# Where the large on-chip tensors begin: a two-layer decoder trunk with its SBUF tensors moved by 128 or 192 bytes

## What is computed

```python
for i in range(DEPTH):                       # DEPTH = 2, layer i
    shift1, scale1, gate1, shift2, scale2, gate2 = split(silu(c) @ w_mod[i] + b_mod[i], 6)
    h = rms_norm(x, g0) * (1 + scale1) + shift1
    y = pool_mixer(h) if i == 0 else diff_attention(h)
    x = x + gate1 * rms_norm(y, g1)
    h = rms_norm(x, g2) * (1 + scale2) + shift2
    if i == 0: y = (silu(h @ w_g) * (h @ w_u)) @ w_down              # width 2816
    else:      y = sum over 8 experts e of gate[e] * swiglu_e(h)      # width 3584 each
    x = x + gate2 * rms_norm(y, g3)
```

## Time and profile before

| | us |
|---|---|
| three runs | 1496.49, 1496.77, 1496.89 (median 1496.77) |
| the profiled execution, device time | 1496.16 |
| its span, first to last instruction | 1493.9 |
| PE busy | 1374.5 (92% of the span) |
| DVE busy | 1204.4 (81%) |
| ACT busy | 891.3 (60%) |
| DMA | 465.12 MB, 311 GB/s over the span |

### The profile page before, as it was taken

How to read it: one execution, slowest core, us unless ns; L and a number is a source line. 1 busy time by engine, 2 the same in 40 slices (tenths; PEclk the granted TensorE clock), 3 DMA queues, 4 the chain that set the end, 5 groups by cost and what they waited for, 6 DMA issues and landing times.

```text
span 1493.9 us, 19719 instructions
## 1 busy us (share of the span) xinstructions
PE 1374.5 (92%) x6868; PEld 1133.7 (76%) x6868; DVE 1204.4 (81%) x951; ACT 891.3 (60%) x726; POOL 46.9 (3%) x56
## 2 busy tenths in 40 slices
PE   0559999989778999999999999999999999999995
PEld 0349999779557888788788878878887887887883
DVE  7777677788767888888888888888888888888883
ACT  1144433444745776676677767667776766766771
POOL 2230000000200000000000000000000000000000
PEclk9969999999988999999999999999999999999998
DMA  9978788859137999999999999999999999999970
GB/s 375 372 235 296 253 308 289 288 191 393 35 115 245 375 368 337 337 365 364 333 337 370 331 335 367 353 335 354 367 333 337 364 335 335 364 368 334 336 294 30
DMA packets 206228, 465.12 MB, mean 311 GB/s; under 512 B 14472, under 2 KB 37072, under 8 KB 206176
## 3 DMA queue, kind: packets, MB, share of 16 engines
q1 hardware_dynamic: 203744, 456.19, 85.1%
q0 software_dynamic: 2432, 8.26, 1.6%
HBM read 463.33 MB, written 1.06 MB: 311 GB/s over the span
## 4 chain that ended last, share of the span: by engine, by line
PE 85%; DVE 8%; issue 2%; DMA 2%; ACT 1%; POOL 1%; POOLq 0%; DVEq 0%; SPq 0%; ACTq 0%
PE ps L1263 26%; PE ps L1265 26%; PE ps L1264 26%; DVE rows L860 2%; PE ps L1503 2%; PE ps L1512 2%; DVE rows L862 2%; PE ps L1529 2%; DMA raw<-w_mod 1%; DVE wlo L848 1%; PE ps L1247 1%; PE ps L1258 1%; ACT whi L584 1%; DVE ysb L922 0%; DVE hs L904 0%
## 5 line engine op out<-in xcount | busy, mean ns | idle before, releaser
L1105 DVE TENSOR_TENSOR wlx<-raw,whx 128x2048 fp32r<-128x2048 f32 x168 | 385.1, 2292 | 119.7 <-ACT whx L753 119.6
L1105 DVE TENSOR_TENSOR wlo<-raw,whi 128x2048 fp32r<-128x2048 f32 x168 | 383.8, 2288 | 23.5 <-ACT whi L753 22.5
L753 ACT ACTIVATE whi<-raw 128x2048 fp32r<-128x2048 f32 x168 | 322.0, 1918 | 123.2 <-PE ps L1265 123.2
L753 ACT ACTIVATE whx<-raw 128x2048 fp32r<-128x2048 f32 x168 | 322.0, 1918 | 90.8 <-PE ps L1265 90.8
L1263 PE MATMUL ps<-whi,thi 128*128 128x512 f32 x516 | 206.8, 401 | 1.4 <-DVE tlo L852 1.4
L1265 PE MATMUL ps<-whi,tlo 128*128 128x512 f32 x516 | 201.5, 391 | 0.0
L1264 PE MATMUL ps<-wlo,thi 128*128 128x512 f32 x516 | 200.8, 389 | 0.0
L1265 PE MATMUL ps<-whx,tlo 128*128 128x512 f32 x444 | 175.2, 395 | 0.0
L1263 PE MATMUL ps<-whx,thi 128*128 128x512 f32 x444 | 174.9, 394 | 0.0
L1264 PE MATMUL ps<-wlx,thi 128*128 128x512 f32 x444 | 174.9, 394 | 0.0
L848 DVE TENSOR_TENSOR wlo<-raw,whi 128x2048 fp32r<-128x2048 f32 x49 | 111.1, 2289 | 43.1 <-ACT whi L584 43.1
(11 more groups left out here) (182 smaller groups left out, 1919.4 us busy)
## 6 DMA issues: line engine op xcount, KB each, us to landing
raw<-moe_w_gu SPq DMA_DIRECT2D x448, 512.0 KB, 5.5
raw<-moe_w_down SPq DMA_DIRECT2D x224, 512.0 KB, 5.7
raw<-w_mod SPq DMA_DIRECT2D x96, 512.0 KB, 6.4
raw<-ffn_w_gu SPq DMA_DIRECT2D x44, 512.0 KB, 5.0
raw<-w_qkv SPq DMA_DIRECT2D x24, 512.0 KB, 6.4
raw<-ffn_w_down SPq DMA_DIRECT2D x22, 512.0 KB, 5.0
gain<-norm_g POOLq DMA_DIRECT2D x8, 512.0 KB, 7.1
raw<-w_o SPq DMA_DIRECT2D x8, 512.0 KB, 8.0
```

Of the source, the lines that this page charges most:

```text
L753: act.activation(m_hi[m % MRING], raw[:, r % RAW, :], ACT.Copy).then_inc(hi_ready, 1)
L1105: dve.tensor_tensor(m_lo[m % MRING], raw[:, r % RAW, :], m_hi[m % MRING].bitcast(F32), ALU.subtract).then_inc(unit_done, 1)
```

## The change

Two tensors that nothing reads or writes are allocated: one of 128 bytes a partition ahead of `raw`, and one of 64 bytes a partition ahead of `rows`.

```diff
+        sb("pad0", [P, 32])
         raw = sb("raw", [P, RAW, UNIT])
         whi = sb("whi", [P, SPL, UNIT], F32R)
...
         top_idx = sb("top_idx", [P, T, 8], U32)
...
+        sb("pad1", [P, 16])
         before_experts = ExitStack()
         rows = early("rows", [P, 7, D])
```

## The result

| | before | changed kernel |
|---|---|---|
| median, us | 1496.74 | 1482.22 (1481.71 to 1483.18) |
| ratio, 95% interval | | 0.9904 (0.9887 to 0.9921) |
| profiled execution: device time, span | 1496.16, 1493.9 | 1481.71, 1479.4 |

The change is faster by 14.5 us. The forecast was 80 us less: 1416.8 us, in a range from 1403 to 1456. The direction held, the size did not.

What follows compares the result with a forecast made beforehand. PE's own matmul pace was taken to bound some 1100 us. Gains of 38.1 + 25.0 + 11.6 + 4.1 + 1.2 = 80.0 us off 1496.16 gave 1416.2, with the median at 1416.8 us; range 1403 to 1456.

Steps and rivals of the forecast that it cites:

- The paces in the rows: PE timeline before: 120.0 ns for 256 columns; for 512 columns 226.9 on whi, wlo and 233.4 on whx, wlx.
- the time on top equals (256 - begin) / 4 columns in both cases: Moving operands: a begin inside a 256-byte block costs 32 columns at 128, 48 at 64, none at 0.
- an aligned pace of 214.5 ns: 512-column matmuls with begin 0: 214.5 ns each, half of a plain float32 matmul; 108 for 256 columns.
- `whx`, `wlx`: 2016 matmuls: Experts: pace falls from 233.4 to 214.5 ns, 18.9 ns a matmul, 38.1 us gained.
- `whi`, `wlo` in the experts: 2016: Experts: pace falls from 226.9 to 214.5 ns, 12.4 ns a matmul, 25.0 us gained.
- dense stage: Dense chunks at 12.0 ns and down matmuls at 12.4: 16.0 us, 11.6 left without three chunks PE doesn't pace.
- q, k, v: Projections: 4.6 us for q and k, 1.2 for v; 4.1 of 5.8 taken, since DVE limits the stretch.
- loads into `raw`: DMA wait of 20.62 us at 26.29: taken as 0, with 1.2 us to gain or lose as bounds.
- Only `whx` gains: Rival, 0.06: 13.3 ns are the price of a float32r matmul, 128 as good as 0; 13 us gained, 1484.
- One block too many: Rival, 0.10: fetch always asks for the block behind the last column, 240.0 ns for 512 columns; slower, 1557.
- The begin is not the cause: Rival, 0.04: whi and whx differ in something else, say where in the partition they lie; 1497.
- DMA or DVE takes over: Rival, 0.08: expert loads can't pass 375 GB/s, ordinary chunks stay at 16.8 us, 35 us lost again; 1452.

Runs made afterwards that it cites:

- the rulers: Changed kernel with ring slots given different begins by longer slots and pads, four kernels, one execution each: 1487.01, 1502.4, 1503.97 and 1489.85 us.
- Ruler A: Changed kernel with whi, wlo slots at 32, 64, 96 and whx, wlx slots at 128, 160, 224, stationary tiles at 0: 1502.4 us.
- The bfloat16 kernels: Experts' split products in bfloat16 instead of float32r, with the changed kernel's begins: 1437.61 us; with the begins of the kernel before: 1435.45 us, ratio 0.9588.

## Why the prediction was wrong in size

**What bounds the kernel: right.** PE still paces the experts, 973.00 of 973.00 us; every nanosecond taken from a matmul on `whx` came off the end: 36 x 6.7 ns are 0.24 us, and a chunk became 0.25 us shorter.

**The paces in the rows: read rightly.** 120.0, 226.7 and 233.3 ns come back in other kernels with the same pairs of begins; only the rulers, which mix several begins, leave them by up to some 4 ns.

**The step that failed: "the time on top equals (256 - begin) / 4 columns in both cases".** 32 columns at a begin of 128 and 48 at 64 fit that, but these are two points, and in both of them a second thing differed as well: `whi` at 128 moves against activations at 128, `whx` at 64 against activations at 128. The rows could not tell "begins at 64" from "begins elsewhere than what it meets", since no tensor of the kernel before had the one without the other. Moving the standing tiles alone told them apart: 233.3 ns with the weights at 0. Ruler A went against the formula at other begins too: it asked for 230.0, 226.7 and 216.7 ns at 96, 128 and 224, and the slots took 234.2, 231.8 and 233.6.

**From it, the value that failed: an aligned pace of 214.5 ns.** It rested on the formula at a begin of 0, outside what the rows held, and on half of a plain float32 matmul. Equal begins give 226.7, which `whi` had before. The terms of the gain, forecast and measured:

| term | forecast, us | measured, us |
|---|---|---|
| `whx`, `wlx`: 2016 matmuls | 18.9 ns, 38.1 | 6.7 ns, 13.5 |
| `whi`, `wlo` in the experts: 2016 | 12.4 ns, 25.0 | 0 |
| dense stage | 12.0 ns, 11.6 | 0 |
| q, k, v | 4.1 | 0 |
| output projection | 1.2 | 0 |
| loads into `raw` | 0, bounds -1.2 to 1.2 | some 1.1 |

**The rivals.** "Only `whx` gains" named the time (1484; measured 1482.2) and had 0.06. Its reason, that 128 is as good as 0, is true as far as it goes: any begin is, if both operands have it. That 13.3 ns are the price of a `float32r` matmul is not: 256 columns have 6.7 ns on top at 113.4. The objection to it in the prediction, that at the half clock the same matmul has nothing on top, did not weigh against it: the plain float32 matmuls, whose columns pass at half the rate too, lose nothing at either of two distances (429 ns at 192 before and at 0 now), so that nothing on top at half the rate says nothing on begins. "One block too many" was excluded by the same run as the forecast. "The begin is not the cause" fell: 64 bytes in the begin of the standing tiles alone move the pace by 6.7 ns. With it fell, for these matmuls, what the prediction drew from the Trainium skill, "SBUF — State Buffer", section on the DMA port swizzle, that with lines of 16 bytes all begins here are alike. "DMA or DVE takes over" could not show in the changed kernel, where PE never came near the forecast pace. The bfloat16 kernels come within 1.3 ns of it, with the same loads and with splits of 2284 to 2291 ns on DVE that write 2 bytes, and PE is still busy almost all the time, at 367 GB/s:

```profile
467.00:1400.00 933.00, 931.58 (x4488) 452.18 (x4487) 840.89 (x515) 693.58 (x478) 0.00 (x0) 1.00 0.98 367
```

So at 215.8 ns neither took over there; at 214.5 in `float32r` it was not tried.

**What the chances should have been.** A formula with nothing fitted, matched by two points, held 0.72. To ask what else differed between the two points would have put "only `whx` gains" beside it, and the range down to 1484.

**The loads.** The term was taken as 0 with 1.2 us for its bounds, and some 1.1 us came; in the second profile of the changed kernel the dense stage is 0.8 us ahead (176.91 for 177.74), so the size is uncertain. The stretch from 26 to 47 us, in kernels with both groups at 128, both at 32, first group at 128 and second at 0, and both at 0 (the changed kernel again):

```profile
26.00:47.00 21.00, 0.00 (x0) 0.00 (x0) 12.92 (x11) 2.19 (x4) 3.02 (x5) 1.00 1.03 398
```
```profile
26.00:47.00 21.00, 0.00 (x0) 0.00 (x0) 12.96 (x11) 2.19 (x4) 3.02 (x5) 1.00 1.02 398
```
```profile
26.00:47.00 21.00, 0.00 (x0) 0.00 (x0) 13.77 (x11) 2.19 (x4) 3.02 (x5) 1.00 1.03 413
```
```profile
26.00:47.00 21.00, 0.00 (x0) 0.00 (x0) 13.47 (x11) 2.19 (x4) 3.03 (x5) 1.00 1.02 420
```

398 GB/s with neither group at a multiple of 256, 413 with one, 420 with both (the last column; the earlier trace rows has 398 and the first run of the changed kernel 418; 413 with 64 and 0 and 412 with 0 and 192 fit in). For these transfers, unlike for PE, the multiple of 256 itself counts, by 5%. In the experts, where loads wait for PE, hardly any of it shows: the DMA engines are busy 0.97 of the time at 348 GB/s before and at 352 now. The Trainium skill, "DMA: Bandwidth & Descriptors", section "How a descriptor splits into AXI transactions", says that transactions of 256 bytes start at multiples of 256, so that a descriptor that starts elsewhere begins with one that is only partly used; it tells this for reading, while here the begins are those of what is written. 17 transactions in place of 16 for 4096 bytes are an estimate of 6% from that page, near the 5% of the trace; counted in the page's beats of 32 bytes the estimate would be 1 to 3%.

**What stays open.** Shown is that a `float32r` matmul loses more or fewer columns by the begin of its moving operand against the stationary one. Not shown is how: why equal begins lose 32 columns at either length and others 36 to 50 at 512 but 16 to 32 at 256, why half as many stationary columns lose more, and why one unit runs at 113.8 ns and another on the same tiles at 117.7. Patterns that repeat unchanged from matmul to matmul (some 229 and 237 ns in turn at a distance of 128) speak against other engines' traffic as the cause; that the two reads meet in one place of SBUF is an argument, not a measurement. Which of the two operands' width makes bfloat16 free of it was not separated, nor were the 2-byte writes of ACT and DVE that come with it.

## What to carry to other kernels

Where PE is the bound and both operands of a matmul are `float32r`, give the tensors that move and the tensors that stand the same begin within 256 bytes, whichever it is, when 512 columns move at a time; 64 bytes of padding were worth some 13 us here. Read the pace as the distance between starts, per pair of tiles, and compare it with the columns at the granted clock; then list everything that differs between a fast and a slow pair before fitting a formula to one of the differences. Big DMA destinations were best at a multiple of 256 bytes, but that paid only where a load was waited for, by about a microsecond.

## What was not expected of the hardware

- The relative begin of a matmul's two operands sets its pace in float32r: 226.7 ns for 512 columns at equal begins, 228.6 to 234.2 at all others tried, already at 8 bytes (high part) and 32 (low part). Behind a unit at another distance the first 3 to 10 matmuls are slow even at equal begins.
- For 256 columns it is the reverse: 120.0 ns at equal begins, 113.4 to 120.1 at others, most of them below 119.
- In bfloat16 the same stream takes 215.8 ns at both arrangements of begins tried; a weight load takes 98 ns there and 188 in float32r.
- Where loads are waited for, DMA moves 417 to 421 GB/s into tensors at a multiple of 256 and 398 into others; splits on DVE (2288 to 2293 ns) and ACT (1918 to 1922) don't mind begins of 0, 32, 64 or 128.
